# RWKV recurrence on one core: a half's front within the levels of the half before, and two preparation steps first

## The reference

```python
def rwkv7_scan(r, decay, k, v, kk, a):
    def step(S, inp):
        r_t, w_t, k_t, v_t, kk_t, a_t = inp
        sa = jnp.einsum('bhvk,bhk->bhv', S, -kk_t)
        S = (S * w_t[:, :, None, :]
             + sa[..., None] * (kk_t * a_t)[:, :, None, :]
             + v_t[..., None] * k_t[:, :, None, :])
        y = jnp.einsum('bhvk,bhk->bhv', S, r_t)
        return S, y
    ...
    _, y = lax.scan(step, S0, xs)
...
y = (y - mean) * lax.rsqrt(var + RWKV_GN_EPS) * ln_w.reshape(H, N) + ln_b.reshape(H, N)
y = y + jnp.sum(r * k * r_k, axis=-1, keepdims=True) * v
y = y.reshape(B, T, RWKV_WIDTH) * jax.nn.silu(gate)
```

## Time and profile before

| | us |
|---|---|
| median of 3 runs | 2508.17 (2503.44 to 2510.92) |
| the profiled execution | 2510.8 |
| its span, first to last instruction | 2509.0 |

### The profile page before, as it was taken

One profiled execution on the slowest core, in us unless ns is written; L12 is line 12 of the kernel. 1 busy time (PEld: TensorE's weight loads), 2 busy tenths in 40 slices (PEclk: granted clock), 3 DMA queues, 4 the chain that ended last, 5 costly groups with the idle time before them and its releaser, 6 DMA issues.

```text
span 2509.0 us, 40772 instructions
## 1 busy us (share of the span) xinstructions
PE 2292.7 (91%) x17697; PEld 1429.9 (57%) x17697; DVE 805.0 (32%) x1691; ACT 549.2 (22%) x1165; POOL 565.1 (23%) x418
## 2 busy tenths in 40 slices
PE   8999997787789999999999979989899989888987
PEld 7888776667555545888886544433334444444432
DVE  4111315663567734223232441221211111111115
ACT  4011213442466622111121320000000000000002
POOL 5333332331110013433331011111111111111110
PEclk9999998998899999999999989999999999999999
DMA  5223210003110032221225239999999999999997
GB/s 201 88 94 134 76 76 29 12 29 119 61 68 1 1 109 69 81 60 34 62 56 205 114 130 385 429 429 429 428 415 427 429 428 430 428 429 430 429 429 295
DMA packets 73945, 538.33 MB, mean 215 GB/s; under 512 B 14152, under 2 KB 16456, under 8 KB 48032
## 3 DMA queue, kind: packets, MB, share of 16 engines
q1 hardware_dynamic: 58464, 507.55, 49.4%
q0 software_dynamic: 10240, 16.82, 1.8%
q10 hardware_dynamic: 5056, 11.28, 1.5%
HBM read 502.55 MB, written 43.52 MB: 218 GB/s over the span
## 4 chain that ended last, share of the span: by engine, by line
PE 71%; DMA 16%; DVE 5%; issue 4%; ACT 3%; POOL 0%; POOLq 0%; SPq 0%; DVEq 0%; ACTq 0%
PE banks L224 44%; DMA arena<-in_wg 15%; PE banks L229 8%; PE banks L231 8%; PE banks L230 8%; PE banks L1682 2%; ACT arena L234 1%; ACT arena L1610 1%; PE banks L2968 1%; DMA arena<-in_wo 0%; DMA h2d<-arena 0%; DVE arena L1116 0%; DVE arena L3272 0%; DVE arena L1588 0%; DMA arena<-in_con 0%
## 5 line engine op out<-in xcount | busy, mean ns | idle before, releaser
L224 PE MATMUL banks<-arena 64*64 64x64 f32 (+10 forms) x14041 | 1568.3, 357 | 151.8 <-DMA arena<-in_wg 52.1
L224 PEld LDWEIGHTS banks<-arena 64*64 64x64 f32 (+2 forms) x14041 | 823.9, 153 | 824.6 <-issue 724.9
L234 ACT ACTIVATE arena<-banks 128x512 f32<-128x512 f32 (+5 forms) x357 | 194.9, 557 | 902.9 <-PE banks L224 535.8
L2962 POOL DMA_INDIRECT yb<-arena x64 | 64.8, 1012 | 789.3 <-DVE arena L3082 771.4
L3082 DVE TENSOR_SCALAR arena<-banks,arena 128x512 f32<-128x512 f32 x64 | 48.1, 751 | 502.4 <-PE banks L224 502.4
L229 PE MATMUL banks<-h1h,w2s 128*128 128x512 f32 x448 | 177.3, 396 | 1.7 <-DVE h1l L1999 1.7
L231 PE MATMUL banks<-h1h,w2s 128*128 128x512 f32 x448 | 174.7, 390 | 0.0
L230 PE MATMUL banks<-h1l,w2s 128*128 128x512 f32 x448 | 174.3, 389 | 0.0
L229 PE MATMUL banks<-hh,wlo 128*128 128x512 f32 x432 | 172.0, 398 | 0.0
L231 PE MATMUL banks<-hh,wlo 128*128 128x512 f32 x432 | 169.6, 393 | 0.0
L230 PE MATMUL banks<-hl,wlo 128*128 128x512 f32 x432 | 168.4, 390 | 0.0
(11 more groups left out here) (262 smaller groups left out, 1758.9 us busy)
## 6 DMA issues: line engine op xcount, KB each, us to landing
arena<-in_wg SPq DMA_DIRECT2D x64, 2048.0 KB, 31.1
arena<-in_wd SPq DMA_DIRECT2D x64, 2048.0 KB, 30.3
arena<-in_wu SPq DMA_DIRECT2D x63, 2048.0 KB, 26.2
arena<-in_w SPq DMA_DIRECT2D x55, 512.0 KB, 3.5
spill<-arena SPq DMA_DIRECT2D x27, 512.0 KB, 2.6
arena<-spill SPq DMA_DIRECT2D x27, 512.0 KB, 5.5
arena<-in_wo SPq DMA_DIRECT2D x16, 512.0 KB, 7.1
arena<-yb SPq DMA_DIRECT2D x8, 1024.0 KB, 12.9
```

The costliest lines, as they stand in the source:

```text
L224: return pe.e.matmul(o, l, r, start=start, stop=stop)
L234: return act.e.activation(o, i, ACT.Copy)
L2962: return pool.e.indirect_dma_start(yb, bass.IndirectOffsetOnAxis(ap=six[:, col:col + 1].bitcast(U32), axis=0), src[:, :], None, bounds_che ...
```

## The change

- `SC` and `TTm` exist twice. The front of a half (score 0, score 1, AB) is issued within the levels of the half before: one part each in levels 2, 3 and 4, between F and T, as a main step of its own on every engine. The front of the next pair's first half so comes in the last levels of this pair.
- Half 0 and the last half (7) keep the front at their own beginning, now in three steps ("late"); the second buffer is not used for half 7, so nothing of it stands within half 6.
- "turned" moves between F and T of level 0, "end" behind T of level 0.
- POOL does the front's work in two parts: with score 1 the identity on A and the transposed copy; with AB the identity on T.
- The last products are regrouped into two PSUM tiles that are filled one after the other, `YQ` (Y and Q) and then `HG`, with the matmuls in the order of `CORNERS`; the second engine to read a tile (DVE) waits for the first (ACT).
- A half now has 19 main steps (half 0 and half 7 three more), and the side string for pairs 0 to 2 begins with P's first two steps and has ten alternations instead of twelve.

```diff
-    SC = sb("SC", [128, 2, 4, 4, 64], c=c2)
-    TTm = sb("TTm", [128, 2, 8, 64], c=c2)
+    SCs = [sb("SC0", [128, 2, 4, 4, 64], c=c2)]
+    TTs = [sb("TTm0", [128, 2, 8, 64], c=c2)]
...
+    SCs.append(sb("SC1", [128, 2, 4, 4, 64], c=c2))
+    TTs.append(sb("TTm1", [128, 2, 8, 64], c=c2))
...
+    def early_half(i, hf):
+
+        n = 2 * i + hf + 1
+        return HALVES[n] if n < LAST_HALF else None
+
+    def late_front(i, hf):
+        return 2 * i + hf in (0, LAST_HALF)
+
+    def wait_buffer(eng, i, hf):
+
+        n = 2 * i + hf
+        before = n - 1 if n == LAST_HALF else n - 2
+        if before >= 0:
+            u = ps["YQ", *HALVES[before]]
+            eng.wait_ge(u.full, u.v)
...
     def pe_main(pe, i):
...
+            if late_front(i, hf):
+                for part in range(3):
+                    pe_front(pe, i, hf, part)
                     yield
...
                     pe_F(pe, i, hf, lv, h)
                 yield
+                if lv == 0:
+                    pe_turned(pe, i, hf)
+                    yield
+                if lv >= 2:
+                    if ahead:
+                        pe_front(pe, *ahead, lv - 2)
+                    yield
...
                     pe_T(pe, i, hf, lv, h)
                 yield
+                if lv == 0:
+                    pe_ends(pe, i, hf)
+                    yield
...
+            u = ps.open(pe, ("YQ", i, hf), ring="main")
             for jj in range(4):
...
+                for h, p in CORNERS:
+                    mm(pe, u.t[H64[h], y[p]], WU[H64[p], h, jj, 64:128], SC[H64[p], h, jj, 1, :], True, False)
+                for h, p in CORNERS:
+                    mm(pe, u.t[H64[h], y[p]], TL[H64[p], jj, 3, H64[h]], SC[H64[p], h, jj, 3, :], False, True)
+                for h, p in CORNERS:
+                    t = mm(pe, u.t[H64[h], q[p]], WU[H64[p], h, jj, 0:64], SC[H64[p], h, jj, 1, :], True, True)
+            t.then_inc(u.full.sem, 1)
             yield
...
     def dve_main(dve, i):
...
                 yield
+                if lv == 0:
+                    yield
+                if lv >= 2:
+                    if ahead:
+                        dve_front(dve, *ahead, lv - 2)
+                    yield
                 evac_T(dve, dve.e.tensor_copy, i, hf, lv, 0)
                 yield
...
+            u = ps["YQ", i, hf]
             dve.wait_ge(u.full, u.v)
+            dve.wait_ge(s("Y_copied"), 2 * i + hf + 1)
...
-    SIDE = ["TT" + "PT" * 12 + "T" * 9] * (NP - 1) + ["T" * 8 + "NT" * 8 + "T" * 20]
+    SIDE = ["PPTT" + "PT" * 10 + "T" * 9] * (NP - 1) + ["T" * 8 + "NT" * 8 + "T" * 20]
```

More of the change, by code:

```diff
@@ L935, in evac_T, with pe_score @@
             copy_(o[:, 0:2 * n].rearrange("p (b n) -> p b n", b=2), two(u)[:, :, 0:n]).then_inc(u.free.sem, 1)
+    CORNERS = ((0, 0), (1, 1), (0, 1), (1, 0))
+    def pe_score(pe, i, hf, g):
+        if hf == 0 and g == 0:
+            for name in ("A", "R", "B", "K"):
+                pe.wait_ge(s(name), i + 1)
+        AR_ = AR[i % 2]
+        u = ps.open(pe, ("score", i, hf, g), ring="main")
+        for jj, p in CHUNKS[4 * g:4 * g + 4]:
+            ts = tokens(hf, jj, p)
+            for kind, left in enumerate((Bt[i % 2], Kt[i % 2])):
+                for h in range(2):
+                    at = 512 * h + 256 * (jj % 2) + 128 * kind
+                    o = u.t[H64[p], at:at + 128].rearrange("p (a n) -> p a n", a=2)
+                    t = mm(pe, o, left[H64[h], ts], AR_[H64[h], :, ts], True, True)
+        t.then_inc(u.full.sem, 1)
@@ new lines, in pe_AB, with pe_front @@
+    def pe_AB(pe, i, hf):
+        u = ps.open(pe, ("AB", i, hf), ring="main")
+        for jj, p in CHUNKS:
+            ts = tokens(hf, jj, p)
+            for h in range(2):
+                at = 512 * h + jj * 64
+                t = mm(pe, u.t[H64[p], at:at + 64], AR[i % 2][H64[h], 0, ts], Bt[i % 2][H64[h], ts], True, True)
+        t.then_inc(u.full.sem, 1)
+    def pe_front(pe, i, hf, part):
+        if part < 2:
+            pe_score(pe, i, hf, part)
+        else:
+            pe_AB(pe, i, hf)
@@ new lines, in pe_turned, with pe_ends @@
+    def pe_turned(pe, i, hf):
+        u = ps.open(pe, ("turned", i, hf), ring="main")
+        for jj in range(4):
+            js = slice((4 * hf + jj) * 128, (4 * hf + jj + 1) * 128)
+            pe.e.transpose(u.t[:, 256 * jj:256 * jj + 128], AR[i % 2][:, 0, js], ident)
+            t = pe.e.transpose(u.t[:, 256 * jj + 128:256 * jj + 256], vq[i % 2][:, js], ident)
+        t.then_inc(u.full.sem, 1)
+    def pe_ends(pe, i, hf):
+        pe.wait_ge(s("D"), i + 1)
+        u = ps.open(pe, ("end", i, hf), ring="main")
+        for kind, left in enumerate((Bt[i % 2], Kt[i % 2])):
+            for jj in range(4):
+                for h, p in CORNERS:
+                    ts = tokens(hf, jj, p)
+                    at = 512 * h + 256 * kind + 64 * jj
+                    t = mm(pe, u.t[H64[p], at:at + 64], left[H64[h], ts], Dn[i % 2][H64[h], ts], True, True)
+        t.then_inc(u.full.sem, 1)
@@ L1122, in dve_main @@
             m1 = C("m1", 0, 64).unsqueeze(1).unsqueeze(1).to_broadcast([128, 2, 4, 64])
-            dve.e.tensor_tensor(TTm[:, :, 0:4, :], two(u)[:, :, 0:256].rearrange("p h (j n) -> p h j n", j=4), m1,
+            dve.e.tensor_tensor(TTs[half_buffer(i, hf)][:, :, 0:4, :], two(u)[:, :, 0:256].rearrange("p h (j n) -> p h j n", j=4), m1,
                                 ALU.mult).then_inc(u.free.sem, 1)
-            yield
-            yield
-            yield
+    def dve_main(dve, i):
+        for hf in range(2):
+            ahead = early_half(i, hf)
+            if late_front(i, hf):
+                for part in range(3):
+                    dve_front(dve, i, hf, part)
+                    yield
             for lv in range(5):
@@ L1155, in dve_main, with pool_front @@
             yield
[L1157 to L1161 removed]
+    def pool_front(pool, i, hf, part):
+        SC, TTm = SCs[half_buffer(i, hf)], TTs[half_buffer(i, hf)]
+        id2 = C("id2", 0, 64).unsqueeze(1)
+        if part == 1:
+            wait_buffer(pool, i, hf)
             u = ps["score", i, hf, 1]
```

209 lines of the change are left out of this document (94 added, 115 removed).

## The result

The changed kernel takes 2523.06 us (median of 7 runs, 2519.84 to 2527.46) against 2508.24 us (7 runs, 2500.06 to 2510.92) before. The ratio is 1.0062, 95% interval 1.0046 to 1.0078: slower, outside the range of the prediction. The profiled execution took 2519.84 us, span 2518.0.

A forecast was written before the change was run, and what follows sets the result against it. TensorE's chain was taken to bound this stage, with waits for GpSimd and DVE. Openings -31.9, rests +21.0, stalls +1.8 and clock +4.5 gave -4.6 us: 2504 us from a median of 2508.17, range 2491 to 2517.

The forecast's parts named there:

- The openings of halves 1 to 5: From each half's start to level 2: shorter by 8.3, 3.9, 6.7, 5.3 and 6.5 us with the front gone.
- I take 1.2: Half 0's opening: waiting for a third GpSimd operation before level 0 adds 1.2 us, between nothing and 2.25.
- +1.0: Half 7's opening: the same wait for a third GpSimd operation, with fewer blocks to cover it, adds 1.0 us.
- +5.3 and +5.4: Halves 3 and 5, level 2 to next start: longer because step 22 (L1275), waiting for GpSimd, precedes level 4's copy.
- -3.4: Half 6's opening: 3.4 us shorter, gaining its front and short waits; its rest unchanged.
- The credit of +1.8: Stalls for "issue" without a partner, credited to the openings, follow instruction count and fall elsewhere: +1.8 us.
- some 2.6: Level 3 of halves 2 and 4: new wait of 2.6 us for DVE's copy behind multiply and k operations.
- The clock term: Four new waits of 2.6 to 3 us, half followed by a low-clock dip, each over half of 4 us: +4.5 us.
- B: Rival: each new wait brings the low clock, four dips of 4 us, with longer tail waits 2517 us; chance 0.15.
- A: Rival: rests bound by TensorE alone, each of six growing by 2.5 us, no dip; 2493 us; chance 0.25.
- C: Rival: last products' neighbours overlap on the array, saving 1.5 us in each of eight halves; 2492 us; chance 0.05.
- D: Rival: the early front waits for its inputs (A, R, B, K of the next pair), 3 us three times; 2513; chance 0.05.

The follow-up runs named there:

- experiment 1: Changed kernel with pair 0's preparation of the next pair begun behind the half's front instead of between its parts: 1.0068 of the kernel before.
- Experiment 5: Changed kernel with halves 0 and 7 put back in the old order of blocks, GpSimd sums and side steps: 0.9994 of the kernel before, 2505.63 us.
- experiment 4: Changed kernel with half 7's two rotary side steps behind the front's three parts instead of between them: 1.0052 of the kernel before.
- experiment 2: Changed kernel with the recurrence's step 22 one slot later, behind level 4's copy, in every pair: 1.0014 of the kernel before, 2509.55 us.
- experiment 3: Changed kernel with the preparation's two operations on k behind level 2's copy in even halves: 1.0068 of the kernel before.
- experiment 11: Changed kernel, halves 0 and 7 in old order, step 22 later, plus even halves' k operations and L801 later: 1.0030 of the kernel before.
- experiment 8: Kernel before with only the last products of each half regrouped as in the change: 0.9994 of the kernel before.
- Experiment 12: Changed kernel with 60 products of overwritten result filling the wait ahead of W and U in halves 3 and 5: 1.0052 of the kernel before.
- experiment 6: Changed kernel with halves 0 and 7 in old order and step 22 one slot later in pairs 1 and 2: 0.9967 of the kernel before, 2500.01 us.
- experiment 9: Changed kernel with 96 products of overwritten result in the wait ahead of W and U in halves 3 and 5: 1.0079 of the kernel before.

## Why the prediction was wrong

The stage came out 12.7 us longer where -10.9 was forecast before the terms for stalls and clock, and -4.6 with them. The openings of halves 1 to 5 and the places of the new waits were right. The step that failed is the opening of halves 0 and 7, "I take 1.2" and "(+1.0)": the prediction took the cover out of their wait and priced it at nothing. They hold 14.2 of the 23.6 us between -10.9 and +12.7. Halves 3 and 5 hold 7.2.

1. **Half 0, "I take 1.2, since these run alone".** It was +9.6. The step priced only GpSimd's third operation. Two things were missed: DVE's first preparation step, moved between the front's multiplies, waits for a load (experiment 1: 6.5 us of the delay of level 0), and the transposes, the "end" products and the preparation, which had lain in the 7.6 us between front and level 0 (the row from 363.67 ends at 366.16, level 0 began at 373.75), went behind level 0. Experiment 5 put both back and took 7.3 us off. Level 0 also ran at the low clock, some 0.9 us. The prediction asked what covers each wait in six halves and not in this one.

2. **Half 7, "+1.0".** It was +6.6, by the same omission; experiment 5 took 6.8 off, the whole of it. Experiments 1 and 4 show that the waits alone are not the loss.

3. **Rests of halves 3 and 5, "+5.3 and +5.4".** The place, the cause and the order were right (experiment 2). The wait was 3.94 us and not about 3: the sum had 1.28 us each for L1270 and L1275, but they took 2.16 and 2.27 (L1356 and L1361 in the rows). Each begins just behind a 1.26 us operation of GpSimd's part of the early front (495.87 and 500.61) and ends about 1.1 us after that one. The early front brought this collision with it. The rows of before had the kind, though not the place: L799 takes 1.76 us where L796 takes 1.23, and the prediction itself priced L1168 "beside a DVE product" at 2.25. Half 7, with no early front, has L1361 at 1.28. On top came the low clock, 1.7 us in half 3 and 2.9 in half 5. A mean of 2.3 us is what the prediction took for one dip ("a little over half of the 4 us"), but it let half of the waits have one, and both of these did. And the prediction's own terms from 571.74 on add up to 7.2 us, not to the 7.45 that it goes on with.

4. **Half 6, "-3.4".** It was -1.9, opening -8.9 and rest +6.9. The first compression block (3.9 us on TensorE, at 603.85 before and 604.28 after) lies ahead of the mark before and behind it after, which explains most of both. W and U waited 1.5 us.

**Half 1** got -4.7 where -6.4 was forecast. Its opening was better than forecast (9.1 us, no wait for GpSimd); its rest was 3.5 us worse, of which 1.8 us is one stall in level 2's products and 1.8 one in the last products. The credit of +1.8 for such stalls covered one of the two. Over the whole stage steps of more than 0.6 us from one matmul's start to the next, with no semaphore to wait for, add up to 16.7 us before and 15.0 after: they wander, they do not grow.

**Halves 2 and 4** were right: -0.4 and -1.9 against -0.5 and -0.9, with the wait at level 3 (2.69 us against "some 2.6"). Experiments 3 and 11 show that it cannot be moved away by order alone.

**The clock term**, +4.5 for four new waits with half of them followed by a dip: of the four, halves 3 and 5 had one, half 4 a short one (the front's score products in it took 2.7 us, in half 2 1.9), half 2 none. That is 1.7, 2.9 and 0.8 us, 5.4 in all: the term was nearly right. What it left out are the waits of halves 0 and 7: behind half 7's 4.61 us the transposes took 1.97 us in all, before 1.09. The prediction also said that both waits of before over 2.3 us were followed by the low level. There was a third of their kind, 2.29 us for GpSimd in half 3 (half 5's was 2.30), ending at 479.66, and behind it the granted clock was 1.00 until 484.9.

**The rivals.** B came nearest, in sign and size (2517, 0.15), but for another reason. Its point of decision, more than two waits each followed by 8 us at 0.50, was not met: behind half 5's wait the clock was at 0.50 for 8.5 us, behind half 3's for 4.3, half 4's 2.9, half 2's none. And the 17.0 us of halves 0 and 7, more than the whole net loss, are in no rival. A fell: the rests of halves 1 to 5 grew by 2.7 to 10.3 us. C fell with experiment 8. D: no front waited for its inputs.

**The nameless stalls** can be named from the traces, which hold the DMA packets too. The queue of the kind "instruction" (q8) moves packets of 16 KB, 142 in a run and about one in 4.6 us in this stage. In the 14 traces TensorE has 140 idle times of over 0.4 us in the stage with no semaphore to wait for, and each of them ends 1.2 to 1.7 us behind the end of such a packet. Of the 603 that long that do have a semaphore to wait for, 69 end at that distance. Experiment 12's 2.9 us one, its row of TensorE and the queue's line of the DMA view for 510 to 520 us (packets, MB, share):

```profile
518.86 1.44 PE L224 MATMUL banks<-arena 64*64 64x64 f32 x34 [2.86 <-issue]
...
q8 instruction: 1, 0.02, 0.6%
```

TensorE stops at 516.00, the packet runs from 516.49 to 517.45, and TensorE goes on at 518.86. So the stalls come with late instructions; this is read from the traces, and no experiment tests it. What makes a packet late is open: this one follows a stretch of 2 us in which DMA was 0.76 busy, but ahead of 85 of the 140 packets the DMA engines had been less than 0.05 busy for 3 us.

**Left open.** Why W and U of half 5 run at the low level in experiments 2 and 6 while those of half 3, with the same rows ahead of them, do not.

## What to carry to other kernels

Before moving blocks out from between a producer and its consumer, list what runs in that gap on every engine, in the first and last iteration as well: a block that is gone from under a wait costs time behind it (up to its full length, as in halves 0 and 7). When a step is moved, follow all of its queues; here one load on DVE's queue, one sum on DVE's behind GpSimd's, and one product on GpSimd's each decided a result. A string of slots is a schedule, and one more slot in an iteration moves every later side step.

## What the runs showed of the hardware

- In these runs a DVE operation on two SBUF operands that starts during a GpSimd operation ends about its own length after that one ends: L801 (L799 in the kernel before) took 1.21 us alone, 1.32 to 1.76 when it began in the last 0.2 to 0.7 us of GpSimd's multiply, 2.94 when it began 0.5 us behind its start; L1361 took 1.28 and 2.27.
- The level of TensorE's clock can differ between two passes over the same sequence: 1.96 and 3.51 us for the same 32 products behind the same 0.55 us wait (experiment 2). With useless products in a wait of 3.9 us it stayed at 1.00, where it had fallen to 0.50 (experiments 9 and 12).
- 64x64 products laid over two corners of the array, every second one in the corner of its neighbour, took 26 ns a record; those over four different corners took 17 (Y and Q: 96 records in 1.63 us). That the corners make the difference was not tested.
- TensorE's instructions come in packets of 16 KB, and when one is late TensorE stalls: 8 to 12 times in this stage of 300 to 327 us, 9 to 20 us in all, each stall ending 1.2 to 1.7 us behind its packet.
